# Moving the second pair of S5 output matmuls into the next unit, and writing the A blocks out

## The chip, the cores and the metric

The kernel runs on one core of one Trainium2 chip, as one program. The metric is device time in microseconds (us), the median of several runs; lower is better. PE is TensorE, DVE VectorE, ACT ScalarE, POOL GpSimd, SP the queue that issues most loads.

## The reference, cut to what matters

One layer of a hybrid decoder on 256 prompt rows and 8 x 8 sample rows, so 320 token columns, with a model width of 4096, all in fp32. One input projection feeds three branches, A (gated convolution), B (RG-LRU) and C (S5); their outputs are concatenated, projected back, gated and added to the input, and a last RMSNorm follows.

```python
proj = h @ w_in
a_b, a_c, a_x, a_g, b_x, b_g, c_u, c_g = _split_cols(proj)
conv_out, conv_a_new = _causal_dwconv(conv_a, a_c * a_x, w_conv_a, b_conv_a)
out_a = a_b * conv_out * jax.nn.silu(a_g)
...
bu_re = jnp.einsum('gpi,btgi->btgp', bb_re, u)      # S5: into 64 complex states per group
bu_im = jnp.einsum('gpi,btgi->btgp', bb_im, u)
...                                                 # diagonal complex scan over time: hr, hi
y = (jnp.einsum('gip,btgp->btgi', s5_c_re, hr) - jnp.einsum('gip,btgp->btgi', s5_c_im, hi)
     + s5_d * u).reshape(bn, t_len, W_C)            # second term: the skip term
y = jax.nn.gelu(y)
y = y * jax.nn.sigmoid(y @ w_glu + b_glu)
out_c = y * jax.nn.silu(c_g)
mixed = jnp.concatenate([out_a, out_b, out_c], axis=-1) @ w_out
```

## The kernel before, in words

Channels lie on the 128 partitions and tokens along the free axis. Each fp32 matmul of a projection is made of three fp32r matmuls (high x high, high x low, low x high). Weights stream in as slabs of 128 x 1024 words through a ring of four. For each slab SP issues the load, ACT copies the high part (`hi`, L575 to L582), DVE subtracts it to get the low part (`lo`, L877 to L880), and PE runs 24 matmuls on it (`slab`, L400 to L419). ACT and DVE prepare slabs three ahead of PE, so in their loops the index c runs from 3 to 18 where PE's runs from 0 to 15. A slab of the old ring place must be finished by PE before ACT may write that place.

The stages are: a head (L470 to L474, written out instruction by instruction: the projections whose results feed B and C, and the conditioning matmuls), then the A stage, then G (the GLU projection of C), B, and O (the output projection).

The change is in the **A stage**. It has eight units u of 16 slabs: two halves h, each with four units m (512 columns each of a_c, a_x, a_b and a_g), u = 4h + m. PE runs it as a loop of eight passes, ACT and DVE as loops of two passes (one per half) with the four units written out inside, POOL likewise. Beside the projection of A, each unit carries the S5 work of 128 channels of C, in four parts j = 0 to 3, t = 4u + j:

- PE, after slabs 1, 3, 6 and 9: six small matmuls into A0[0] and A0[1] (L488 to L490). The first of a unit waits for `bbu_ready`, the split operands UU_LO and BBU_LO that DVE writes at its c = 3 (L1111, L1112).
- DVE, at c = 5, 7, 10 and 13: `turn` (L1065 to L1081), which rotates by cosine and sine tables, and runs two scans; it ends with `q_done`.
- POOL, in order of t: six products and sums (L1337 to L1342) that rotate back into HRI[j % 2] and end with `hs5_done`; then a copy to the staged state and `frac` (L1296 to L1300), the fractions from which ACT makes the tables of part t + 2. Before HRI is written again, `y_done` must show that PE has read it. At the end of a unit POOL stores the state and waits for the store (L1351); for m = 2 it also stores the convolution state (L1355). At m = 2, before its last part, it waits for `conva_done` and copies that state (L1332, L1333). At the start of a unit it waits for `y_done` of all earlier pairs and loads CC, the output matrices (L1325). At the start of a half it first waits for `ag_done` and fills PADA's borders (L1290, L1291, `pada_ready`).
- PE, after slab 8 (parts 0 and 1) and after slab 15 (parts 2 and 3): the **output matmuls** (L501, two instructions for each of four fp32 matmuls) into A0[2]. Each pair waits for its `hs5_done`; the first also for `cc_ready` (ACT has negated the imaginary half, L694) and `y_sum` (DVE has read A0[2] of the unit before).
- DVE, after its last slab of the unit: waits for `y_done` of the second pair and adds the skip term (L1123, L1124, `y_sum`).

For the A branch, ACT evacuates the four banks at the unit's end (L720 to L725). DVE runs the convolution in four `conv_a` calls at m = 2, c = 4, 8, 11 and 14 (L1083 to L1097), and two products at m = 3. In a half's last unit, ACT at c = 5 waits for `y_sum` and runs GELU over three finished rows of C and SiLU over four gate rows (L704, L706). DVE begins a half with a wait for `pada_ready`.

After the A stage, G's first slab on PE waits for Y_LO, which DVE writes once `frac_done` has reached 34, that is after POOL's last `frac` (L1130 to L1138).

Within the two-pass loops the wait values and the column addresses depend on h, so they come from registers; outside they are constants.

Of the kernel before, what the change touches and what calls it, by code (L numbers as in the profile page):

```python
# [47 lines left out]
N_A, N_G, N_O = 8, 2, 8  # L48
# [17 lines left out]
SW = TP + DB * (DS + 1)  # L66
# [6 lines left out]
C_BRG, C_BIG, C_LAM, C_BGLU, C_S5D, C_GF = 240, 256, 272, 288, 296, 304  # L73
# [35 lines left out]
def build(nc, a):  # L109
    ctx = ExitStack()  # L110
    with ctx:
# [71 lines left out]
        CC = at("s5_cc", s + 2048, 2, BLK, 32)  # L183
# [213 lines left out]
        def _(pe):  # L397
# [76 lines left out]
                pairs(n)  # L474


            with pe.Fori(0, N_A) as u:
                for c in range(SPG):
                    slab(SLAB_A + u * SPG, c, KT, Q_A + u, H_HI, H_LO, T, after_head=True)
                    if c in (1, 3, 6, 9):  # L480
                        j = c // 3
                        if j == 0:
                            pe.wait_ge(bbu_ready, u + 1)
                        pe.wait_ge(bu_used, 4 * u + j + 1)
                        r = slice(32 * j, 32 * j + 32)
                        for n in range(2):
                            out = A0[n][:, 0:SW]
                            mm(out, BBU_HI[r, n, :], UU_HI[r, :], start=True, stop=False)  # L488
                            mm(out, BBU_HI[r, n, :], UU_LO[r, :], start=False, stop=False)
                            last = mm(out, BBU_LO[r, n, :], UU_HI[r, :], start=False, stop=True)  # L490
                        last.then_inc(bu_done, 1)
                    if c in (8, 15):
                        pair = c // 15
                        if pair == 0:
                            pe.wait_ge(cc_ready, u + 1)
                            pe.wait_ge(y_sum, u + 1)
                        pe.wait_ge(hs5_done, 4 * u + 2 * pair + 2)
                        for n in range(2):
                            for par in range(2):
                                j = 2 * pair + par  # L500
                                last = mm(A0[2][32 * j:32 * j + 32, 0:SW], CC[:, n, j, :], HRI[par][:, n, :],  # L501
                                          start=n == 0, stop=n == 1)
                        last.then_inc(y_done, 1)


            with pe.Fori(0, N_G) as g:
# [61 lines left out]
        def _(act):  # L568
            fn = nc.scalar.activation
            st = act_step  # L570
# [106 lines left out]
            tables(0, 0)  # L677
            act.wait_ge(hdv_free, N_H - HSL)
            act.wait_ge(ada_used, CHUNKS * KT)
            with act.Fori(0, 2) as h:  # L680
                st.enter(h, 32)
                for m in range(4):
                    u = 4 * h + m
                    nb = SLAB_A + u * SPG
                    q = Q_A + u
                    for c in range(AHEAD, AHEAD + SPG):
                        if c == 3:
                            act.wait_ge(bu_done, 4 * u + 1)
                            fn(UU_HI[:], CST[:, u, :], ACT.Copy)
                            fn(BBU_HI[:], BB[:, u], ACT.Copy).then_inc(bbu_hi_done, 1)  # L690
                        hi(nb, c)
                        if c == 5:
                            act.wait_ge(cc_in, 16 * (u + 1))
                            fn(CC[:, 1], CC[:, 1], ACT.Copy, scale=-1.0).then_inc(cc_ready, 1)  # L694
                        if c in (3, 6, 9, 12):
                            j = c // 3 - 1
                            act.wait_ge(q_done, 4 * u + j + 1)
                            fn(COEF[:], MASK[:], ACT.Copy, scale=MAGF[:, 0, bass.ds(4 * u + j, 1)]).then_inc(
                                coef_done, 1)
                        if m == 3 and c == 5:  # L700
                            act.wait_ge(y_sum, 4 * h + 3 + 1)
                            act.sem_inc(act_passed, 1)
                            rows = CST[:, bass.ds(4 * h, 3), :]
                            fn(rows, rows, ACT.Gelu_apprx_tanh)  # L704
                            rows = SG[:, bass.ds(4 * h, 4), :]
                            fn(rows, rows, ACT.Silu).then_inc(silu_done, 1)  # L706
                        if c in (6, 9, 12, 15):
                            j = c // 3 - 2
                            tables((j + 1) % 2, 4 * u + j + 1)
                    for b in range(BLK):  # L710
                        if b == 0 and m == 0:
                            act.wait_ge(pada_ready, h + 1)
                        if b == 0 and m == 2:
                            act.wait_ge(conva_done, h + 1)
                            act.wait_ge(staged_a, h + 1)
                        if b == 0 and m == 3:
                            act.wait_ge(ab_done, h + 1)
                        bank_ready(q, b, nb + SPG)
                        if m == 0:
                            fn(PADA[:, b, 2:2 + TP], M[:, b, 0:TP], ACT.Copy)  # L720
                            fn(PADAS[:, b, :, 2:], MS[:, b], ACT.Copy).then_inc(bank_free, 1)
                        elif m == 1:
                            fn(AROW[:, 4 * h + b, :], M[:, b, 0:T], ACT.Copy).then_inc(bank_free, 1)
                        else:
                            fn(TMPA[:, b, :], M[:, b, 0:T], ACT.Copy).then_inc(bank_free, 1)  # L725
                act.wait_ge(bank_free, 4 * (Q_A + 4 * h + 3) + 8)
                fn(TMPA[:], TMPA[:], ACT.Silu).then_inc(silu_a_done, 1)
            st.leave(2)


            act.wait_ge(silu_done, 2)
# [135 lines left out]
        def _(dve):  # L867
# [15 lines left out]
            def col(c):  # L883

                return PAR[:, bass.ds(c, 1)] if not isinstance(c, int) else PAR[:, c:c + 1]
# [213 lines left out]
                    then(ins)  # L1099


            with dve.Fori(0, 2) as h:
                st.enter(h, 16 * 4 + 4 * 4 - 1)
                dve.wait_ge(pada_ready, h + 1)
                for m in range(4):
                    u = 4 * h + m
                    nb = SLAB_A + u * SPG
                    for c in range(AHEAD, AHEAD + SPG):
# [6 lines left out]
                            conv_a(h, c // 3 - 1)  # L1115
                        if c in (5, 7, 10, 13):
                            turn(4 * u + c // 3 - 1, (c // 3 - 1) % 2)
                        if m == 3 and c == 4:
                            dve.wait_ge(conva_done, h + 1)
                            dve.wait_ge(bank_free, freed(Q_A + 4 * h + 2, 3))  # L1120
                            rows = AROW[:, bass.ds(4 * h, BLK), :]
                            tt(rows, rows, TMPA[:], MUL).then_inc(ab_done, 1)
                    dve.wait_ge(y_done, 2 * u + 2 + 1)  # L1123
                    stt(CST[:, u, :], CST[:, u, :], col(C_S5D + u), A0[2][:, 0:SW], MUL, ADD).then_inc(y_sum, 1)  # L1124
                    if m == 3:
                        dve.wait_ge(ab_done, h + 1)
                        dve.wait_ge(silu_a_done, h + 1)
                        rows = AROW[:, bass.ds(4 * h, BLK), :]
                        tt(rows, rows, TMPA[:], MUL).then_inc(ag_done, 1)
            st.leave(2)  # L1130


            dve.wait_ge(staged_s, 8)
# [387 lines left out]
```

## Time and profile before

| what | value |
|---|---|
| median of 3 runs | 2037.04 us (2034.55 to 2037.42) |
| the profiled execution | 2038.62 us, span 2037.0 us, mean granted clock 0.977 |
| PE busy | 1932.3 us (95% of the span) |
| DVE, ACT, POOL busy | 1133.0, 809.6, 430.6 us (56%, 40%, 21%) |
| DMA | 472.25 MB, mean 232 GB/s |
| chain that ended last | PE 79%, POOL 6%, issue 5%, DVE 5%, DMA 3% |

PE is the engine to watch: what PE waits for, and what a wait then does to the granted clock, is what stands between this kernel and a shorter one. The chain of work that ended last is nearly all PE, but 6% of it lies on POOL, which is busy for 21% of the span only, all of it between 644 and 1206 us (the A stage). A time on a row is the start in us from the span's start; the bracket at its end is how long the engine had been idle and what ended that.

### The profile page before, as it was taken

How to read it: one execution, taken by the hardware profiler on the slowest of the kernel's cores; microseconds unless marked ns; L12 is line 12 of the kernel's file. 1: busy time of each engine (PE TensorE's matmuls, PEld its weight loads, DVE VectorE, ACT ScalarE, POOL GpSimd, SP SyncE). 2: the span in 40 equal slices, each digit the busy share in tenths (PEclk: the TensorE clock that was granted, in tenths of full speed). 3: DMA queues.
4: the chain of work that ended last, by engine and by line, in shares of the span. 5: the costliest groups of instructions: out<-in, count | busy, mean ns of one | idle time of the engine just before them, and what ended most of it. 6: DMA issues, size and time to landing. Idle time of an engine off the chain costs nothing.

```text
span 2037.0 us, 37797 instructions
## 1 busy us (share of the span) xinstructions
PE 1932.3 (95%) x14410; PEld 1758.1 (86%) x14410; DVE 1133.0 (56%) x1535; ACT 809.6 (40%) x1076; POOL 430.6 (21%) x499
## 2 busy tenths in 40 slices
PE   4899999999999999899999889999989999999995
PEld 0688888888888999798998889999978899899995
DVE  2556667555454767776669656655743323333444
ACT  2343323322223444344444445677743223323332
POOL 1000000000001776676676660000000000000000
PEclk9899999999999999899999999999989999999998
DMA  9999999999997443333442434544467767677543
GB/s 388 375 374 353 365 356 352 344 350 344 351 365 296 128 138 133 116 117 128 138 135 96 138 129 160 170 159 158 140 225 262 273 234 273 238 272 258 176 145 124
DMA packets 132054, 472.25 MB, mean 232 GB/s; under 512 B 15424, under 2 KB 18432, under 8 KB 131920
## 3 DMA queue, kind: packets, MB, share of 16 engines
q1 hardware_dynamic: 125712, 448.38, 61.2%
q0 software_dynamic: 4480, 16.01, 2.1%
q10 hardware_dynamic: 1728, 6.07, 0.8%
q8 instruction: 84, 1.38, 0.3%
q14 instruction: 50, 0.41, 0.1%
HBM read 461.68 MB, written 8.72 MB: 231 GB/s over the span
## 4 chain that ended last, share of the span: by engine, by line
PE 79%; POOL 6%; issue 5%; DVE 5%; DMA 3%; ACT 1%; POOLq 0%; DVEq 0%; SPq 0%; ACTq 0%
PE m L414 16%; PE m L415 15%; PE m L416 15%; PE m L458 8%; PE m L459 7%; PE m L460 7%; PE aux L428 6%; DMA ada<-in_ada 3%; PE aux L556 2%; PE aux L520 1%; POOL s_tmpp L1341 1%; POOL s_tmpp L1338 1%; PE aux L501 1%; DVE w_lo L880 1%; POOL sin L1297 1%
## 5 line engine op out<-in xcount | busy, mean ns | idle before, releaser
L414 PE MATMUL m<-h_hi,w_hi 128*128 128x320 f32 x2560 | 809.4, 316 | 14.5 <-issue 9.7
L415 PE MATMUL m<-h_lo,w_hi 128*128 128x320 f32 x2560 | 796.0, 311 | 0.0
L416 PE MATMUL m<-h_hi,w_lo 128*128 128x320 f32 x2560 | 795.9, 311 | 0.0
L880 DVE TENSOR_TENSOR w_lo<-w_raw,w_hi 128x1024 fp32r<-128x1024 f32 x325 | 414.2, 1293 | 497.7 <-ACT w_hi L582 497.0
L582 ACT ACTIVATE w_hi<-w_raw 128x1024 fp32r<-128x1024 f32 x325 | 339.7, 1055 | 540.8 <-PE m L416 540.3
L414 PEld LDWEIGHTS m<-h_hi,w_hi 128*128 128x128 f32 x2560 | 485.5, 190 | 52.1 <-issue 42.6
L415 PEld LDWEIGHTS m<-h_lo,w_hi 128*128 128x128 f32 x2560 | 485.8, 190 | 0.8
L416 PEld LDWEIGHTS m<-h_hi,w_lo 128*128 128x128 f32 x2560 | 485.4, 190 | 0.0
L458 PE MATMUL m<-h_hi,w_hi 128*128 128x320 f32 x1024 | 324.1, 316 | 6.2 <-DVE h_lo L935 6.2
L460 PE MATMUL m<-h_hi,w_lo 128*128 128x320 f32 x1024 | 317.3, 310 | 0.0
L459 PE MATMUL m<-h_lo,w_hi 128*128 128x320 f32 x1024 | 317.3, 310 | 0.0
L597 ACT ACTIVATE w_hi<-w_raw 128x1024 fp32r<-128x1024 f32 x131 | 138.8, 1060 | 339.9 <-PE m L460 332.5
L458 PEld LDWEIGHTS m<-h_hi,w_hi 128*128 128x128 f32 x1024 | 193.0, 188 | 33.4 <-issue 32.2
L459 PEld LDWEIGHTS m<-h_lo,w_hi 128*128 128x128 f32 x1024 | 193.1, 189 | 0.0
L460 PEld LDWEIGHTS m<-h_hi,w_lo 128*128 128x128 f32 x1024 | 193.1, 189 | 0.0
L893 DVE TENSOR_TENSOR w_lo<-w_raw,w_hi 128x1024 fp32r<-128x1024 f32 x131 | 160.4, 1225 | 57.5 <-ACT w_hi L597 57.1
L428 PE MATMUL aux<-ada,c_T 128*32 128x256 f32 x2304 | 152.8, 400 | 30.6 <-DMA ada<-in_ada 30.6
L428 PEld LDWEIGHTS aux<-ada,c_T 128*32 128x32 f32 x2304 | 66.2, 111 | 97.6 <-DMA ada<-in_ada 41.5
L1307 POOL DMA_DIRECT2D part_b<-b_x x8 | 4.5, 566 | 606.2 <-DVE b_x L948 606.2
L947 DVE TENSOR_TENSOR b_x<-b_x,m 128x512 f32<-128x512 f32 x56 | 38.5, 688 | 103.0 <-PE m L460 102.9
L1407 POOL DMA_DIRECT2D x<-in_x x8 | 4.3, 534 | 330.5 <-PE m L416 330.5
L556 PE MATMUL aux<-gate_ring,c_T 128*32 128x256 f32 x768 | 52.5, 390 | 8.8 <-DMA gate_ring<-in_ada 8.8
(251 smaller groups left out, 1664.8 us busy)
## 6 DMA issues: line engine op xcount, KB each, us to landing
w_raw<-in_w SPq DMA_DIRECT2D x456, 512.0 KB, 4.6
ada<-in_ada SPq DMA_DIRECT2D x288, 512.0 KB, 6.4
gate_ring<-in_ada SPq DMA_DIRECT2D x96, 512.0 KB, 5.5
x_head<-in_x ACTq DMA_DIRECT2D x8, 640.0 KB, 13.7
x<-in_x POOLq DMA_DIRECT2D x8, 640.0 KB, 5.6
out_y<-x SPq DMA_DIRECT2D x6, 640.0 KB, 3.5
part_b<-b_x POOLq DMA_DIRECT2D x8, 344.0 KB, 6.2
pad_b<-part_b POOLq DMA_DIRECT2D x4, 688.0 KB, 5.4
```

The source lines that it names most:

```text
L414: mm(out, w_hi, hi[:, k, :], start=k == 0, stop=False)
L415: mm(out, w_hi, lo[:, k, :], start=False, stop=False)
L416: last = mm(out, w_lo, hi[:, k, :], start=False, stop=k == nk - 1)
L428: last = mm(A0[bank][32 * r:32 * r + 32, 0:CW], CT[:, k, :], ADAX[slot][:, r, :], start=k == 0, stop=k == KT - 1)
L458: mm(out, w_hi, H_HI[:, k, :], start=kk == 0, stop=False)
L459: mm(out, w_hi, H_LO[:, k, :], start=False, stop=False)
L460: last = mm(out, w_lo, H_HI[:, k, :], start=False, stop=kk == HK - 1)
L556: last = mm(A0[0][32 * r:32 * r + 32, 0:CW], CT[:, k, :], ADA2[:, k % RING, r, :], start=k == 0, stop=k == KT - 1)
L582: fn(W_HI[:, c % RING], RAW[:, c % RING].rearrange("p (k n) -> p k n", k=2), ACT.Copy).then_inc(w_hi_done, 1)
L597: fn(W_HI[:, w_slot(n)], RAW[:, n % RING].rearrange("p (k n) -> p k n", k=2), ACT.Copy).then_inc(w_hi_done, 1)
L880: tt(W_LO[:, c % RING], RAW[:, c % RING].rearrange("p (k n) -> p k n", k=2), W_HI[:, c % RING].bitcast(F32), SUB).then_inc(w_lo_done, 1)
L893: tt(W_LO[:, w_slot(n)], RAW[:, n % RING].rearrange("p (k n) -> p k n", k=2), W_HI[:, w_slot(n)].bitcast(F32), SUB).then_inc(w_lo_done, 1)
```

## The change

Three edits. (1) PE's loop over the eight units is written out, and the second pair of output matmuls of unit u goes from behind slab 15 of unit u to behind slab 1 of unit u + 1, just ahead of that unit's first S5 input matmuls; the last unit's stays at the end. (2) What depends on it follows: DVE adds the skip term of unit u - 1 at c = 5 of unit u, after `turn`; ACT negates CC at c = 7 (was 5); GELU and SiLU come at c = 8 (was 5). (3) ACT's and DVE's two-pass loops are written out, so that their wait values and addresses are constants; POOL keeps its loop.

```diff
+            def s5_in_(u, j):
+                if j == 0:
+                    pe.wait_ge(bbu_ready, u + 1)
+                pe.wait_ge(bu_used, 4 * u + j + 1)
...
+                last.then_inc(bu_done, 1)
+            def s5_out(u, pair):
+                if pair == 0:
+                    pe.wait_ge(cc_ready, u + 1)
+                    pe.wait_ge(y_sum, u + 1)
+                pe.wait_ge(hs5_done, 4 * u + 2 * pair + 2)
...
+                last.then_inc(y_done, 1)
-            with pe.Fori(0, N_A) as u:
+            for u in range(N_A):
                 for c in range(SPG):
                     slab(SLAB_A + u * SPG, c, KT, Q_A + u, H_HI, H_LO, T, after_head=True)
+                    if c == 1 and u > 0:
+                        s5_out(u - 1, 1)
                     if c in (1, 3, 6, 9):
-                        j = c // 3
...
-                    if c in (8, 15):
-                        pair = c // 15
...
+                        s5_in_(u, c // 3)
+                    if c == 8:
+                        s5_out(u, 0)
+            s5_out(N_A - 1, 1)
@@ ACT
-            with act.Fori(0, 2) as h:
-                st.enter(h, 32)
+            for h in range(2):
...
-                        if c == 5:
+                        if c == 7:
                             act.wait_ge(cc_in, 16 * (u + 1))
                             fn(CC[:, 1], CC[:, 1], ACT.Copy, scale=-1.0).then_inc(cc_ready, 1)
...
-                        if m == 3 and c == 5:
+                        if m == 3 and c == 8:
                             act.wait_ge(y_sum, 4 * h + 3 + 1)
-                            act.sem_inc(act_passed, 1)
                             rows = CST[:, bass.ds(4 * h, 3), :]
                             fn(rows, rows, ACT.Gelu_apprx_tanh)
@@ DVE
+            def add_skip(u):
+                dve.wait_ge(y_done, 2 * u + 2 + 1)
+                stt(CST[:, u, :], CST[:, u, :], col(C_S5D + u), A0[2][:, 0:SW], MUL, ADD).then_inc(y_sum, 1)
-            with dve.Fori(0, 2) as h:
-                st.enter(h, 16 * 4 + 4 * 4 - 1)
+            for h in range(2):
...
                         if c in (5, 7, 10, 13):
                             turn(4 * u + c // 3 - 1, (c // 3 - 1) % 2)
+                        if c == 5 and u > 0:
+                            add_skip(u - 1)
...
-                    dve.wait_ge(y_done, 2 * u + 2 + 1)
-                    stt(CST[:, u, :], CST[:, u, :], col(C_S5D + u), A0[2][:, 0:SW], MUL, ADD).then_inc(y_sum, 1)
+                    if u == N_A - 1:
+                        add_skip(u)
```

## Rows read from the trace of the kernel before

**Rows 1.** Waits of PE: line, releaser, total us, times, longest us.
```profile
PE aux L501 <- POOL s_h__104 L1342: 14.8, 8, 5.2
...
PE m L414 <- issue: 9.7, 2, 4.9
...
PE m L414 <- DVE y_lo L1137: 4.7, 1, 4.7
PE aux L488 <- DVE s_bb_unit_lo L1112: 3.5, 2, 3.0
```
**Rows 2.** Timeline of PE, end of unit 2: start, duration, line, tiles, idle before.
```profile
852.02 0.31 PE L416 MATMUL m<-h_hi,w_lo 128*128 128x320 f32 x1
857.20 0.76 PE L501 MATMUL aux<-s_h__103,s_cc 128*32 128x328 f32 x1 [4.87 <-POOL s_h__104 L1342]
...
859.53 0.63 PE L414 MATMUL m<-h_hi,w_hi 128*128 128x320 f32 x1
```
**Rows 3.** Windows: PE, PEld, DVE, ACT, POOL busy us (instructions), clock, DMA.
```profile
855.00:860.00 5.00, 2.80 (x10) 1.03 (x11) 0.24 (x1) 0.00 (x0) 3.88 (x9) 0.50 0.18 74
```
**Rows 4.** Timeline of PE, ends of units 0 and 1.
```profile
719.78 0.46 PE L501 MATMUL aux<-s_h__103,s_cc 128*32 128x328 f32 x1 [0.54 <-POOL s_h__104 L1342]
...
721.01 0.41 PE L414 MATMUL m<-h_hi,w_hi 128*128 128x320 f32 x1
...
784.09 0.46 PE L501 MATMUL aux<-s_h__103,s_cc 128*32 128x328 f32 x1
...
785.32 0.42 PE L414 MATMUL m<-h_hi,w_hi 128*128 128x320 f32 x1
```
**Rows 5.** Timeline of POOL from unit 2 into unit 3.
```profile
847.21 1.07 POOL L1332 COPY stage_a<-pad_a 128x36 f32<-128x36 f32 x1 [6.53 <-DVE acts L1093]
...
856.27 0.87 POOL L1342 TENSOR_TENSOR s_h__104<-s_h__104,s_tmpp 128x328 f32<-128x328 f32 x1 [0.18 <-POOL s_tmpp L1341]
...
867.27 0.54 POOL L1325 DMA_DIRECT2D s_cc<-in_s5c  x1 [3.27 <-DMA out_o_ca<-stage_a]
875.09 0.90 POOL L1337 TENSOR_TENSOR s_h__103<-q,cos 128x328 f32<-128x328 f32 x1 [7.28 <-DVE q L1081]
```
**Rows 6.** Timeline of POOL from unit 6 into unit 7.
```profile
1142.35 0.54 POOL L1325 DMA_DIRECT2D s_cc<-in_s5c  x1 [3.32 <-DMA out_o_ca<-stage_a]
1150.80 0.89 POOL L1337 TENSOR_TENSOR s_h__103<-q,cos 128x328 f32<-128x328 f32 x1 [7.91 <-DVE q L1081]
```
**Rows 7.** Timeline of DVE inside a convolution call of unit 2.
```profile
830.55 0.95 DVE L1089 TENSOR_SCALAR acts<-pad_a,par 128x256 f32 x1 [0.20 <-DVE pad_a L1088]
```
**Rows 8.** Timeline of DVE and PE, first S5 part of unit 3.
```profile
867.62 0.41 PE L488 MATMUL aux<-s_u_unit_hi,s_bb_unit_hi 32*128 32x328 f32 x1
...
868.72 0.41 PE L414 MATMUL m<-h_hi,w_hi 128*128 128x320 f32 x1
...
873.99 0.82 DVE L1081 TENSOR_TENSOR_SCAN q<-s_coef,q 128x328 f32<-128x328 f32 x1
```
**Rows 9.** Timelines of POOL, DVE, PE and ACT where the halves meet.
```profile
922.79 1.64 POOL L1342 TENSOR_TENSOR s_h__104<-s_h__104,s_tmpp 128x328 f32<-128x328 f32 x1 [0.18 <-POOL s_tmpp L1341]
...
935.15 0.50 DVE L1111 TENSOR_TENSOR s_u_unit_lo<-acts,s_u_unit_hi 128x328 fp32r<-128x328 f32 x1 [7.25 <-POOL pad_a L1291]
...
936.04 0.42 PE L488 MATMUL aux<-s_u_unit_hi,s_bb_unit_hi 32*128 32x328 f32 x1 [3.02 <-DVE s_bb_unit_lo L1112]
...
928.38 1.28 ACT L689 ACT_TABLE_LOAD   x1 [2.66 <-issue]
```
**Rows 10.** Timelines of POOL and PE at the end of the A stage.
```profile
1198.78 1.64 POOL L1342 TENSOR_TENSOR s_h__104<-s_h__104,s_tmpp 128x328 f32<-128x328 f32 x1 [0.18 <-POOL s_tmpp L1341]
...
1204.40 0.88 POOL L1300 TENSOR_TENSOR sin<-sin,cos 128x328 f32<-128x328 f32 x1 [0.18 <-POOL cos L1299]
...
1206.45 0.64 PE L414 MATMUL m<-y_hi,w_hi 128*128 128x328 f32 x1 [4.68 <-DVE y_lo L1137]
```
**Rows 11.** DMA queues of the page: packets, MB, share of 16 engines.
```profile
q8 instruction: 84, 1.38, 0.3%
```

More of the change, by code:

```diff
@@ L474, in _ @@
                 pairs(n)
-            with pe.Fori(0, N_A) as u:
+            def s5_in_(u, j):
+                if j == 0:
+                    pe.wait_ge(bbu_ready, u + 1)
+                pe.wait_ge(bu_used, 4 * u + j + 1)
+                r = slice(32 * j, 32 * j + 32)
+                for n in range(2):
+                    out = A0[n][:, 0:SW]
+                    mm(out, BBU_HI[r, n, :], UU_HI[r, :], start=True, stop=False)
+                    mm(out, BBU_HI[r, n, :], UU_LO[r, :], start=False, stop=False)
+                    last = mm(out, BBU_LO[r, n, :], UU_HI[r, :], start=False, stop=True)
+                last.then_inc(bu_done, 1)
@@ new lines, in s5_out @@
+            def s5_out(u, pair):
[3 more added lines that the diff above has]
+                pe.wait_ge(hs5_done, 4 * u + 2 * pair + 2)
+                for n in range(2):
+                    for par in range(2):
+                        j = 2 * pair + par
+                        last = mm(A0[2][32 * j:32 * j + 32, 0:SW], CC[:, n, j, :], HRI[par][:, n, :],
+                                  start=n == 0, stop=n == 1)
+                last.then_inc(y_done, 1)
@@ L478, in _ @@
+            for u in range(N_A):
                 for c in range(SPG):
                     slab(SLAB_A + u * SPG, c, KT, Q_A + u, H_HI, H_LO, T, after_head=True)
+                    if c == 1 and u > 0:
+                        s5_out(u - 1, 1)
                     if c in (1, 3, 6, 9):
-                        j = c // 3
[L482 to L491, printed above, removed]
-                    if c in (8, 15):
-                        pair = c // 15
[L494 to L503, printed above, removed]
+                        s5_in_(u, c // 3)
@@ L727, in _ @@
                 fn(TMPA[:], TMPA[:], ACT.Silu).then_inc(silu_a_done, 1)
-            st.leave(2)
             act.wait_ge(silu_done, 2)
@@ L1129, in _ @@
                         tt(rows, rows, TMPA[:], MUL).then_inc(ag_done, 1)
-            st.leave(2)
             dve.wait_ge(staged_s, 8)
```

## The prediction

> **What bounds the kernel now.** I read the list of PE's waits first, since PE is busy for 95% of the span. A wait of PE matters when nothing else would have held PE at that place a little later. The largest entry on which this change acts is L501, the output matmuls, which wait 14.8 us in eight places for POOL's last sum of a part [rows 1]. The timelines show where: 4.9 us at the end of unit 2, 5.2 at the end of unit 6 (the longest of the list), 0.54 at the end of unit 0, and nothing at the end of unit 1, where the first L501 follows the last slab without a bracket [rows 1, 2, 4]. So the two m = 2 units carry 10 of the 14.8 us, and what they lose is more than the bracket: in the window behind the wait the granted clock is 0.50, that is 1.2 GHz instead of 2.4, and an L501 takes 0.76 us instead of 0.46 [rows 2 to 4].
>
> Second, the timeline of POOL, because POOL ends those waits. In unit 2 POOL stands still for 6.5 us until DVE's last convolution call is done, then copies the convolution state and starts its last part at once [rows 5]. That ends at 857.14, and PE follows at 857.20. Then comes what decides the size of the gain: POOL stores two results, issues the load of CC at 867.27, and is free at 867.81; but it starts unit 3 only at 875.09, after 7.3 us of waiting for DVE's `turn` [rows 5]. That `turn` waited for PE's first S5 matmuls (L488 at 867.62), which come two slabs behind the pair that had waited for POOL [rows 2, 8]. So **PE waits for POOL, and POOL then waits for PE**: a ring through PE, DVE and POOL, closed once per m = 2 unit. Unit 7 shows it again: free at 1142.89, started at 1150.80 [rows 6].
>
> Third, the place where the halves meet. POOL ends unit 3 at 924.43; fractions, a store and PADA's borders follow, DVE waits for the borders, and PE's first S5 matmuls of unit 4 start at 936.04, after 3.0 us of waiting [rows 9]. From 924.43 to 936.04 it is 11.6 us. At the end of the stage POOL ends its last part at 1200.42 and its last fraction at 1205.28, and G's first matmul starts at 1206.45 [rows 10]: 6.0 us after the part. In both places POOL's end of the last part, and not PE's last slab, sets what follows.
>
> **The change, part by part.** The sum is made against the profiled execution, 2038.62 us (its span and 1.6 us around it); the median of the three runs is 2037.04, 1.6 lower, so the gain is then taken from the median.
>
> *The pair behind slab 1 of the next unit.* It is the same number of matmuls; a pair without a wait takes 784.09 to 785.32, 1.23 us, wherever it stands [rows 4]. What goes is the wait ahead of it. A unit without waits takes 721.01 to 785.32, 64.3 us [rows 4]; less four input groups of 1.10 [rows 8] and two pairs of 1.23 this is 57.4 for 16 slabs, so two slabs are 7.2 us. After unit 2 PE would go on at 852.2 (one step of 0.15 behind the row at 852.02) instead of 859.53 [rows 2], reach the pair at 859.4, and find POOL's part done at 857.14: no wait, with 2.2 us to spare. Unit 6 has the same pattern. At unit 0 the 0.54 us goes [rows 4].
>
> What is late next is POOL's own path, so the gain isn't 4.9 us plus the slow clock, but what POOL's start in unit 3 gains. POOL is free at 867.81, or 867.3 with the 0.5 of unit 0. DVE's `turn` must be done as well: PE starts unit 3 at 851.7, two slabs 7.2, the pair 1.2, and from L488 to the end of the second scan 874.81 - 867.62 = 7.2 [rows 8], gives 867.3. The two arrive together. So POOL starts at 867.3 instead of 875.1: **7.8 us, 0.5 of them from unit 0, 7.3 from unit 2**. From there to unit 4's first S5 matmuls the path is POOL's own, four parts (875.09 to 924.43, 49.3 us) and 11.6 us [rows 5, 9], and moves as a whole. The 3.0 us of L488 therefore stays: PE reaches that place at 851.7 + 64.3 + 8.4 = 924.4 plus what unit 3's first pair waits, POOL allows it at 867.3 + 49.3 + 11.6 = 928.2. Units 4 and 5 are PE's pace, so unit 6 gets the 7.8 us passed on. There POOL is free 7.9 us before its start [rows 6]; its last part, and with it G's start, moves by **7.9 us** more.
>
> *What follows on ACT and DVE.* The skip term at c = 5 stands behind `turn`, which already waited for L488; `y_done` is older by then, so it adds no wait, and its one instruction leaves the unit's end. Queued behind it on DVE are the low parts of later slabs, which PE needs three slabs on. `y_sum` comes later, but its readers are the first pair at slab 8 and GELU, which is moved to c = 8, after slab 4. CC's load now waits for the later `y_done`: unit 3's comes at 859.4 + 1.2 = 860.6, POOL asks at 867.27 [rows 5]; in units without a delay it is equally early or just in time. The negation at c = 7 instead of 5 gives CC's transfer two slabs more. GELU, SiLU and their table loads go from ahead of slab 6's high part to ahead of slab 9's, three slabs before PE wants it: nothing. If those covers went, each would cost at most one slab, 3.6 us, once per half.
>
> *Constants instead of registers.* In unit 2 DVE's path from its first `turn` to its last convolution call is what POOL waits for [rows 5]. Before each group that takes an address from a register there is a small gap, 0.20 us in a row where DVE depends on itself alone [rows 7]. Three calls with four such places and three `turn`s with one lie on the path: 15 places. At 0 to 0.20 us each this is 0 to 3.0 us per half; I take 0.1 each less one, **1.4 us per half, 2.8 in all**, since the nearest row has the largest of the gaps in a call. It counts fully, as POOL's last part, its stores and unit 3 move with it.
>
> *The written-out loops.* DVE's and ACT's jumps go. ACT's shows 2.66 us of issue before its first work of unit 4 [rows 9], but DVE was held by POOL's borders until 935.15 [rows 9], and POOL keeps its loop: worth nothing here, at most 2.7 us once. The Trainium skill ("Runtime: NRT & Kernel Launch", Instruction fetch mechanics) says that a taken branch to a target outside the two fetched pages stalls the engine until they are loaded, and prefers unrolling. By that rule alone the change would gain these 2.7 us; by the row of DVE it gains none of them, and the sum keeps none.
>
> Sum: 0.5 + 7.3 + 7.9 + 2.8 = 18.5 us. Profiled execution 2038.6 - 18.5 = 2020.1; median 2037.0 - 18.5, **2018.5 us**.
>
> **The rivals.** (a) *DVE and POOL slow each other.* The same POOL sum takes 0.87 us in one place and 1.64 in another [rows 5, 9]. A unit has 24 such products and sums; if the new phase makes half of them as slow as the slow one, 12 x 0.77 = 9.2 us are lost per half, and nothing is gained: 2037. Half of that gives 2028. For it: POOL now starts unit 3 when DVE has a denser queue. Against: both POOL's start and `turn` keep their distance to PE's slabs within a microsecond. The Trainium skill ("SBUF — State Buffer", Who interferes with whom) says that a DVE instruction with two SBUF inputs and a GpSimd one that reads SBUF exclude each other for a whole instruction; that speaks against bringing POOL's parts closer to DVE's `turn` and low parts, most of which read two SBUF tiles. The two durations agree with it; by it each meeting costs POOL the rest of a DVE instruction, which is what the 0.77 us price.
>
> (b) *POOL's start in unit 3 doesn't move*, because something other than `turn` holds it that the wait list hides behind it. Then only 0.5 us and part of the constants are won, about 1 to 2 us: 2035.5, no change. Against it: the bracket names DVE's scan both times [rows 5, 6].
>
> (c) *Slower: straight-line code on PE has to be fetched.* Two of PE's waits are for "issue", 4.9 us each [rows 1]. If each of the seven further units paid one such reload, 34 us would be lost: 2018.5 + 34 = 2053. It decides from 18.5 / 7 = 2.6 us per unit. Against it: the head runs thousands of matmuls written out, and the list has no issue wait of its matmuls; the instruction queue moves 1.38 MB in 84 packets, 0.3% of the DMA time [rows 1, 11].
>
> (d) *More than forecast*: all of the registers' 3.0 us per half, ACT's 2.7, and a shorter wait at L488, which takes its slow clock with it (3 us): 18.5 + 3.2 + 2.7 + 3 gives 2009.6.
>
> **How the numbers follow.** Forecast, 2012 to 2024: 0.70. Rival (a), 2024 to 2033 in the main: 0.14. (b): 0.06. (c): 0.04. (d), below 2012: 0.06. The range 2010 to 2028 takes the forecast, most of (d) and the better half of (a). A difference of 0.2%, 4.1 us, is about what a measurement of this kernel can tell from no change. Slower by more: (c), 0.04. Same: (b) and the worst of (a), 0.08. Faster: 0.88.
>
> **What would show it.** Right: no wait of L501 at a second pair but the last; L501 of unit 2 behind unit 3's slab 1 without a bracket and at 0.46 us; POOL's first part of units 3 and 7 within 0.5 us of the end of its CC load; the 3 us at unit 4's L488 still there. The constants are right if POOL's 6.5 us before L1332 ends 1 to 2 us earlier relative to unit 2's first `turn`. Wrong: POOL's 49.3 us for four parts of unit 3 grown (a); a bracket with DVE's scan of 5 us or more still at POOL's first part (b); "issue" between PE's slabs of the A stage (c).

## The result, and the profile after

| what | before | after |
|---|---|---|
| median | 2037.23 us (4 runs, 2034.55 to 2037.77) | 2014.29 us (4 runs, 2013.91 to 2015.75) |
| ratio, after to before | | 0.9885, 95% interval 0.9873 to 0.9897 |
| the profiled execution | 2038.62 us, span 2037.0 | 2015.75 us, span 2014.2 |
| mean granted clock | 0.977 | 0.982 |
| first S5 matmul of unit 0 to G's first matmul | 545.3 us | 521.0 us |

By the medians the change gains 22.9 us, by the ratio 23.4 (21.0 to 25.9). 18.5 us were forecast; the time lies in the range, 2010 to 2028. In the kernel after, L485 to L487 are the input matmuls (before: L488 to L490), L499 the output matmuls (L501), L1336 the load of CC (L1325), L1343 the copy of the convolution state (L1332), L1348 to L1353 POOL's six products and sums of a part (L1337 to L1342), L1308 the first wide operation of a fraction, 128x328 (L1297), L591 and L886 the high and low part of a slab (L582, L880).

PE's waits, kernel after (line, releaser, total us, times, longest us), which answer [rows 1]:

```profile
PE m L414 <- issue: 10.3, 2, 5.5
...
PE m L414 <- DVE y_lo L1148: 4.6, 1, 4.6
PE aux L485 <- DVE s_bb_unit_lo L1122: 4.0, 1, 4.0
PE aux L499 <- POOL s_h__104 L1353: 3.9, 6, 1.4
```

The output matmuls wait 3.9 us instead of 14.8. Gone too is a wait that [rows 1] leaves out, for DVE's low parts (kernel before):

```profile
PE m L414 <- DVE w_lo L880: 4.8, 4, 2.1
```

It stood in units 2 and 6 alone, 2.1 and 2.7 us. The waits at unit 4's first input matmuls and at G's first matmul stay, and so do the two of 5 us for issue, which stand in the O stage. (POOL's busy time before is not all in the A stage, as said at the start: 387 of its 431 us are.)

Timeline of PE, kernel after: the end of unit 2's second pair, now behind slab 1 of unit 3; the start of unit 4; the end of the stage. It answers [rows 2, 9, 10].

```profile
851.79 0.31 PE L416 MATMUL m<-h_hi,w_lo 128*128 128x320 f32 x1
852.02 0.46 PE L499 MATMUL aux<-s_h__103,s_cc 128*32 128x328 f32 x1
...
853.25 0.41 PE L485 MATMUL aux<-s_u_unit_hi,s_bb_unit_hi 32*128 32x328 f32 x1
...
917.99 0.44 PE L499 MATMUL aux<-s_h__104,s_cc 128*32 128x328 f32 x1
922.38 0.64 PE L485 MATMUL aux<-s_u_unit_hi,s_bb_unit_hi 32*128 32x328 f32 x1 [3.95 <-DVE s_bb_unit_lo L1122]
...
1175.51 0.46 PE L499 MATMUL aux<-s_h__103,s_cc 128*32 128x328 f32 x1 [1.37 <-POOL s_h__104 L1353]
...
1181.38 0.64 PE L414 MATMUL m<-y_hi,w_hi 128*128 128x328 f32 x1 [4.57 <-DVE y_lo L1148]
```

The pair of unit 2 has no bracket and takes 0.46 us instead of 0.76. Behind it the granted clock is now full, 2.4 GHz, where it was 0.50 in [rows 3] (window, kernel after: PE, PEld, DVE, ACT, POOL busy us, clock, DMA):

```profile
850.00:855.00 5.00, 5.00 (x33) 3.76 (x32) 4.11 (x5) 1.06 (x1) 4.45 (x3) 1.00 0.67 207
```

Timeline of POOL, kernel after, from unit 2 into unit 3 and from unit 6 into unit 7, which answers [rows 5, 6]:

```profile
838.50 1.07 POOL L1343 COPY stage_a<-pad_a 128x36 f32<-128x36 f32 x1 [0.96 <-DVE acts L1099]
...
847.18 0.94 POOL L1353 TENSOR_TENSOR s_h__104<-s_h__104,s_tmpp 128x328 f32<-128x328 f32 x1 [0.18 <-POOL s_tmpp L1352]
...
849.86 2.86 POOL L1308 TENSOR_SCALAR sin<-s_step,s_turn 128x328 f32<-128x328 f32 x1 [0.21 <-POOL s_turn L1307]
...
862.02 0.54 POOL L1336 DMA_DIRECT2D s_cc<-in_s5c  x1 [2.16 <-DMA out_o_ca<-stage_a]
862.58 0.90 POOL L1348 TENSOR_TENSOR s_h__103<-q,cos 128x328 f32<-128x328 f32 x1
...
1126.00 0.54 POOL L1336 DMA_DIRECT2D s_cc<-in_s5c  x1 [2.14 <-DMA out_o_ca<-stage_a]
1126.56 0.90 POOL L1348 TENSOR_TENSOR s_h__103<-q,cos 128x328 f32<-128x328 f32 x1
```

Behind its CC load POOL goes on at once, twice: the waits of 7.3 and 7.9 us are gone, so the ring is open. Two other things are new. POOL waits only 0.96 us for the last convolution call, where it waited 6.53. And from the end of unit 2's last part (848.12) to the end of the CC load (862.56) it takes 14.4 us, where it took 10.7.

**Where the time went.** Each stretch runs from PE's first input matmul of one unit to that of another, in profiled executions (us). The last stretch ends at G's first matmul.

| stretch | forecast | before | after | gain |
|---|---|---|---|---|
| unit 0 to 2 | 0.5 | 131.4 | 128.5 | 2.9 |
| unit 2 to 4 | 8.7 (7.3 + 1.4) | 143.5 | 133.6 | 9.9 |
| unit 4 to 6 | 0 | 131.7 | 130.4 | 1.2 |
| unit 6 to G | 9.3 (7.9 + 1.4) | 138.8 | 128.6 | 10.2 |
| A stage | 18.5 | 545.3 | 521.0 | 24.3 |
| ahead of the stage | 0 | 661.1 | 660.3 | 0.8 |
| behind the stage | 0 | 830.6 | 832.8 | -2.2 |

The stretches ahead of and behind the stage hold no edit. Over all kernels of this study they lie between 659.4 and 663.9, and between 827.9 and 832.8, so a difference of some 4 us there shows no effect of an edit.

### The profile page after: what moved, and what is told of

It reads as the page before. It is cut to its first block, busy times and chain, and to the rows that moved or that the text cites. A ratio compares the mean times of both kernels' runs of the same rounds, so it can differ in the third digit from the quotient of the medians.

```text
span 2014.2 us, 36924 instructions
## 1 busy us (share of the span) xinstructions
PE 1925.7 (96%) x14410; PEld 1754.6 (87%) x14410; DVE 1128.4 (56%) x1535; ACT 803.1 (40%) x1072; POOL 451.5 (22%) x499
## 4 chain that ended last, share of the span: by engine, by line
PE 79%; DVE 6%; POOL 6%; issue 4%; DMA 3%; ACT 1%; POOLq 0%; SPq 0%; DVEq 0%; ACTq 0%
PE m L414 15%; PE m L416 15%; PE m L415 15%; PE m L458 8%; PE m L460 8%; PE m L459 8%; PE aux L428 6%; PE aux L565 2%; DMA ada<-in_ada 2%; DVE w_lo L886 1%; POOL sin L1308 1%; PE aux L529 1%; POOL s_tmpp L1352 1%; POOL s_tmpp L1349 1%; DVE x L1279 1%
## 5 line engine op out<-in xcount | busy, mean ns | idle before, releaser
L886 DVE TENSOR_TENSOR w_lo<-w_raw,w_hi 128x1024 fp32r<-128x1024 f32 x325 | 419.3, 1308 | 505.2 <-ACT w_hi L591 504.7
L591 ACT ACTIVATE w_hi<-w_raw 128x1024 fp32r<-128x1024 f32 x325 | 339.5, 1055 | 538.7 <-PE m L416 538.5
```

The lines of the kernel that those rows point to most:

```text
L591: fn(W_HI[:, c % RING], RAW[:, c % RING].rearrange("p (k n) -> p k n", k=2), ACT.Copy).then_inc(w_hi_done, 1)
L886: tt(W_LO[:, c % RING], RAW[:, c % RING].rearrange("p (k n) -> p k n", k=2), W_HI[:, c % RING].bitcast(F32), SUB).then_inc(w_lo_done, 1)
```

## The experiments

The theory was a ring (PE waits for POOL, POOL then for PE) that opens when the pair moves, plus a small gain of constants on DVE's path. The rivals put it elsewhere: in the constants, in contention, in PE's code. The kernel after was timed beside a median of 2037.23. Those with only PE's loop, with both loops of ACT and DVE, with the move alone and with the followers put back ran beside one further set of runs of the kernel before (median 2038.81), the other three beside another (2036.75); ratios are to these. The last five columns are from the profiled executions, in us. Each is a single execution: the kernel before and the one with PE's loop written out, whose times agree, differ by 2.3 us in the A stage and by up to 1.5 in a stretch, so gains of 1 to 2 us in one stretch are not shown by these columns alone.

| kernel | median us | ratio (95%) | A stage | 0 to 2 | 2 to 4 | 4 to 6 | 6 to G |
|---|---|---|---|---|---|---|---|
| before | 2037.23 | | 545.3 | 131.4 | 143.5 | 131.7 | 138.8 |
| PE loop written out | 2036.01 | 0.9991 (0.9981 to 1.0001) | 543.0 | 131.4 | 143.3 | 131.0 | 137.3 |
| DVE loop written out | 2032.52 | 0.9975 (0.9965 to 0.9985) | 537.9 | 132.9 | 139.1 | 132.9 | 133.1 |
| ACT and DVE loops written out | 2028.90 | 0.9955 (0.9938 to 0.9971) | 534.8 | 131.4 | 137.9 | 132.7 | 132.8 |
| the move, loops kept | 2022.94 | 0.9925 (0.9909 to 0.9942) | 529.5 | 129.8 | 135.7 | 129.4 | 134.5 |
| after, negation and GELU at c = 5 | 2025.17 | 0.9938 (0.9918 to 0.9958) | 531.8 | 128.5 | 139.2 | 129.8 | 134.3 |
| after | 2014.29 | 0.9885 (0.9873 to 0.9897) | 521.0 | 128.5 | 133.6 | 130.4 | 128.6 |
| after, POOL written out | 2001.85 | 0.9820 (0.9804 to 0.9836) | 513.8 | 128.2 | 128.9 | 128.2 | 128.5 |
| the same, shorter POOL path | 2002.76 | 0.9822 (0.9805 to 0.9838) | 509.1 | 128.2 | 128.2 | 128.2 | 124.4 |

### Only ACT's and DVE's loops written out

```diff
-            with act.Fori(0, 2) as h:
-                st.enter(h, 32)
+            for h in range(2):
...
-            with dve.Fori(0, 2) as h:
-                st.enter(h, 16 * 4 + 4 * 4 - 1)
+            for h in range(2):
```

> The kernel before, with ACT's and DVE's two-pass loops written out (constant waits and addresses) and nothing moved; PE keeps its loop and its order. Ring theory (PE waits for POOL at the end of an m = 2 unit, POOL then waits for PE): the ring stays, only DVE's path in units 2 and 6 gets about 2 us shorter each and unit 0 some 2 us: 2037 - 6 = 2031, with the wait ahead of L501 at the end of unit 2 still 3 us or more and POOL still waiting 6 us or more for DVE's scan at the start of unit 3. Rival (the written-out loops are the larger share of the 22.9 us gained): 2025 or less.

Measured: 2028.90 us, 9.2 us by the ratio, against 2.8 of the forecast. The ring is still there, as the timelines of POOL and PE of this kernel show:

```profile
842.45 1.07 POOL L1327 COPY stage_a<-pad_a 128x36 f32<-128x36 f32 x1 [0.96 <-DVE acts L1090]
...
861.81 0.54 POOL L1320 DMA_DIRECT2D s_cc<-in_s5c  x1 [2.95 <-DMA out_o_ca<-stage_a]
869.48 0.89 POOL L1332 TENSOR_TENSOR s_h__103<-q,cos 128x328 f32<-128x328 f32 x1 [7.12 <-DVE q L1078]
```
```profile
852.04 0.46 PE L501 MATMUL aux<-s_h__103,s_cc 128*32 128x328 f32 x1 [3.07 <-POOL s_h__104 L1337]
```

PE still waits 3.1 us for POOL, and POOL 7.1 us for PE's next input matmuls by way of DVE. The waits of the output matmuls for POOL as a whole are no less than the 14.8 us before:

```profile
PE aux L501 <- POOL s_h__104 L1337: 15.2, 13, 3.1
```

The second pairs of the six units other than 2 and 6 now wait 1.0 to 1.4 us each, where three of them waited 0.5 before and three not at all. That goes against what is won in units 0 to 2 and 4 to 6, which gain nothing here. In the kernel after, where the pair is moved, none of them waits but the last.

What the constants did is to shorten DVE's path in unit 2: from the first input matmul to the end of the last convolution call it is 54.5 us before, 49.8 here, 49.5 after. That is 4.7 us and not 1.4. The three convolution calls on the path give 2.8 of it and the four `turn`s 1.7 (21.4 to 19.7 us). The w_lo waits of PE are gone here and with DVE's loop alone written out, while 3.6 us of them stay with the move alone. The next two views show the calls.

DVE's operations of the convolution calls in unit 2, 785 to 847 us, by form (busy us, mean ns | idle before), kernel before:

```profile
L1089 DVE TENSOR_SCALAR acts<-pad_a,par 128x256 f32 x4 | 2.5, 619 | 0.8 <-DVE pad_a L1088 0.8
...
L1090 DVE TENSOR_SCALAR acts<-pad_a,par 128x64 f32 x4 | 1.8, 451 | 0.0
L1088 DVE TENSOR_TENSOR pad_a<-pad_a,acts 128x64 f32<-128x64 f32 x4 | 1.6, 392 | 0.0
```

The same three of the kernel after:

```profile
L1095 DVE TENSOR_SCALAR acts<-pad_a,par 128x256 f32<-128x256 f32 x4 | 1.7, 430 | 0.1
L1096 DVE TENSOR_SCALAR acts<-pad_a,par 128x64 f32<-128x64 f32 x4 | 1.2, 299 | 0.0
...
L1094 DVE TENSOR_TENSOR pad_a<-pad_a,acts 128x64 f32<-128x64 f32 x4 | 0.9, 213 | 0.0
```

The idle time falls from 0.8 to 0.1 us, but the operations themselves become shorter too, the small TENSOR_TENSOR from 392 to 213 ns. Beside POOL a whole call takes 6.6 us before and 4.9 after; the first call of the unit, which has no POOL beside it, takes 3.07 and 2.66, so the gaps alone are 0.4 us a call. The other 1.3 us appear only beside POOL, and are read here as time in which a DVE instruction stood behind one of POOL. The other side of that exchange is POOL's (kernel before, the one with DVE's loop alone written out, and after, over the A stage; columns as above):

```profile
L1297 POOL TENSOR_SCALAR sin<-s_step,s_turn 128x328 f32<-128x328 f32 x32 | 29.9, 935 | 7.5 <-POOL s_turn L1296 7.5
```
```profile
L1295 POOL TENSOR_SCALAR sin<-s_step,s_turn 128x328 f32<-128x328 f32 x32 | 48.7, 1521 | 7.5 <-POOL s_turn L1294 7.5
```
```profile
L1308 POOL TENSOR_SCALAR sin<-s_step,s_turn 128x328 f32<-128x328 f32 x32 | 57.9, 1810 | 7.5 <-POOL s_turn L1307 7.5
```

The fraction's first wide operation takes up to twice as long: a DVE without gaps leaves POOL waiting while POOL's own gaps stay (7.5 us in all three). All nine kernels fall in line: 765 to 936 ns in the three where DVE and POOL both have loops, 1520 to 1810 in the four where POOL alone has one, 862 and 905 in the two where neither has. In unit 2 that cost nothing in front of the last part, because POOL had 6.5 us of waiting there; 0.96 of them are left. The Trainium skill ("SBUF — State Buffer", Who interferes with whom) says that the ports that DVE and GpSimd share are an exclusive lock, and that the order of issue, not the shape of the operation, decides who blocks. The rows agree: with only DVE's loop written out the same instructions changed from 392 to 214 ns on the one engine and from 935 to 1521 on the other.

### Only DVE's loop written out

```diff
-            with dve.Fori(0, 2) as h:
-                st.enter(h, 16 * 4 + 4 * 4 - 1)
+            for h in range(2):
```

> The kernel before with DVE's two-pass loop alone written out; ACT's and PE's loops kept, nothing moved. If the gain of the run with constants on both engines (9 us) sits on DVE, since its path from the first rotation to the last convolution call of unit 2 is what POOL waits for: 2028 to 2031, and the convolution calls beside POOL take 4.9 us instead of 6.6. If ACT's register work or its jump carries it: 2034 or more.

Measured: 2032.52 us, 5.1 by the ratio, somewhat less than expected. DVE's path in unit 2 is 49.7 us, all of the shortening. So some 3 to 4 of the 9.2 us are ACT's (by the medians 3.6, in the A stage 3.1). Timeline of ACT in unit 0, this kernel, where ACT keeps its loop:

```profile
669.06 0.57 ACT L698 ACTIVATE s_coef<-s_mask,s_mag_turn 128x328 f32<-128x328 f32 x1 [2.54 <-DVE q L1081]
669.64 1.28 ACT L671 ACT_TABLE_LOAD   x1
670.94 0.48 ACT L671 ACTIVATE cos<-sin 128x328 f32<-128x328 f32 x1
```

And with ACT's loop written out as well:

```profile
668.54 0.57 ACT L697 ACTIVATE s_coef<-s_mask,s_mag_turn 128x328 f32<-128x328 f32 x1 [1.44 <-DVE q L1078]
669.01 0.46 ACT L671 ACTIVATE cos<-sin 128x328 f32<-128x328 f32 x1
```

As a loop, ACT's code loads a table of 1.28 us ahead of the first cosine of each half (here, and at 941.20 in unit 4) and another at its start (L689); written out, none of these stands there. The load stands ahead of a slab's high part, so DVE's `turn` of the second part comes later too: its scan ends 20.2 us after PE's first input matmul here (680.76 - 660.54), and 17.2 with ACT written out (678.29 - 661.05). Unit 0's **first** pair, which waits 2.1 us for POOL in the kernel before, waits 1.45 with DVE's loop alone written out and 0.20 with ACT's as well; after the change it waits 0.19. The Trainium skill ("ScalarE activation tables: per-element evaluation and per-set limits", Table sets in the compiler and the runtime) says that the back end places the table loads per block. The rows agree: a load of L671 in each half while the loop is a block of its own, and none there when it isn't.

### Only the move, loops kept

In this kernel ACT and DVE keep their two-pass loops, so the second pairs of units 3 and 7, each the last of a half, stay at their unit's end.

```diff
-                    if c == 1 and u > 0:
+                    if c == 1 and u % 4 > 0:
                         s5_out(u - 1, 1)
...
-            s5_out(N_A - 1, 1)
+                if u % 4 == 3:
+                    s5_out(u, 1)
...
-            for h in range(2):
+            with act.Fori(0, 2) as h:
+                st.enter(h, 32)
```

> The changed kernel with ACT's and DVE's two-pass loops kept, so waits and addresses come from registers again; PE is written out; the pairs of units m = 0 to 2 stand behind slab 1 of the next unit, that of m = 3 stays at its unit's end with its skip term. Ring theory: the move alone is worth the forecast 15 to 16 us (0.5 + 7.3 + 7.9): 2021, and together with the gain of the run with constants alone it gives about the whole 22.9. Rival (the written-out loops are the larger share): 2027 or more.

Measured: 2022.94 us, 15.3 by the ratio, where the forecast's terms for the move give 15.7. POOL starts unit 3 directly behind the CC load, as predicted (timeline of POOL):

```profile
866.49 0.54 POOL L1342 DMA_DIRECT2D s_cc<-in_s5c  x1 [2.15 <-DMA out_o_ca<-stage_a]
867.05 0.91 POOL L1354 TENSOR_TENSOR s_h__103<-q,cos 128x328 f32<-128x328 f32 x1
```

So the move opens the ring without the constants. That 867.05 lies so near the 867.3 of the prediction is luck, though: this execution comes to unit 2's first input matmul 3.1 us earlier than the one before (PE's timelines, this kernel, then before).

```profile
789.47 0.41 PE L485 MATMUL aux<-s_u_unit_hi,s_bb_unit_hi 32*128 32x328 f32 x1
```
```profile
792.55 0.41 PE L488 MATMUL aux<-s_u_unit_hi,s_bb_unit_hi 32*128 32x328 f32 x1
```

Counted from that matmul, POOL's start moves by 5.0 us (82.5 to 77.6), where 7.3 were forecast. The wait of 7.3 is gone, but POOL's last part of unit 2 takes 9.9 us instead of 7.7, and the two small copies behind it 1.25 and 1.19 instead of 0.21 and 0.19. The windows of that last part show what stands beside it (before, then this kernel; length first, then the columns of [rows 3]):

```profile
849.44:857.14 7.70, 2.88 (x20) 2.62 (x18) 2.96 (x2) 4.17 (x9) 7.16 (x7) 0.84 0.77 268
```
```profile
845.45:855.32 9.87, 9.62 (x66) 9.35 (x64) 8.96 (x7) 5.11 (x10) 9.34 (x7) 1.00 0.75 246
```

Before, PE stood still for most of it and DVE was busy for 3.0 of the 7.7 us; now PE goes on, and DVE is busy for 9.0 of 9.9. So the ring's wait had also kept DVE out of POOL's way, and that goes with it. In unit 6 the part and the copies are as slow, and the two stores are waited for 2.3 us longer as well (3.75 and 3.92 us, before 2.07 and 3.32), so POOL's start moves by only 2.2 us of 7.9.

The stretches show the same. Units 2 to 4 gain 7.8 us (7.3 forecast), of which 2.6 are unit 3's four parts, shorter than before (49.3 to 46.8); unit 6 to G gains only 4.2 (7.9 forecast); and units 0 to 2 and 4 to 6 together gain 3.8, for which 0.5 was forecast. So the 15.3 meet the 15.7 by misses that cancel. With the constants, 15.3 + 9.2 = 24.5 against 23.4 for both, within the intervals; by stretches the two do not simply add (units 2 to 4: 7.8 + 5.6 against 9.9).

### The followers put back

```diff
-                        if c == 7:
+                        if c == 5:
                             act.wait_ge(cc_in, 16 * (u + 1))
...
-                        if m == 3 and c == 8:
+                        if m == 3 and c == 5:
```

> The changed kernel with ACT's negation of CC back at c = 5 and GELU and SiLU back at c = 5; all else as changed. If the followers matter: in units 3 and 7 POOL asks for CC at 862 while PE is already at slab 2, so ACT, held at c = 5 until CC lands some 3 us later and then by 4.9 us of GELU and SiLU, gives slab 6's high part about 3 us late; PE waits there, the tables of the second part come late and POOL with them: 3 to 5 us per half, 2020 to 2024. If only the place of the pair matters: 2014.

Measured: 2025.17 us, 10.8 of the 23.4 us lost. Timelines of ACT and PE in unit 3, this kernel:

```profile
864.47 0.31 ACT L702 ACTIVATE s_cc<-s_cc 128x128 f32<-128x128 f32 x1 [11.13 <-DMA s_cc<-in_s5c]
864.80 1.28 ACT L711 ACT_TABLE_LOAD   x1
...
869.63 1.04 ACT L591 ACTIVATE w_hi<-w_raw 128x1024 fp32r<-128x1024 f32 x1
```
```profile
871.98 0.62 PE L414 MATMUL m<-h_hi,w_hi 128*128 128x320 f32 x1 [1.91 <-DVE w_lo L886]
...
888.69 0.44 PE L499 MATMUL aux<-s_h__103,s_cc 128*32 128x328 f32 x1 [2.87 <-POOL s_h__104 L1353]
```

With the negation at c = 5, ACT stands 11.1 us for CC's load, which POOL issues only after its stores, and then makes GELU and SiLU (4.8 us) before it may go on with a slab. PE waits 1.9 us for that slab. The larger loss is behind it: DVE's `turn` of part 1 stands behind the late low part, its scan ends at 879.7 instead of 871.1, POOL's second part ends 5.9 us later (888.5 against 882.6) with everything on POOL's path behind it, and the first pair waits 2.9 us. In the kernel after, the negation waits 2.05 us for the same load and GELU stands ahead of a slab that isn't due yet. The two moves were not taken apart, so which of them carries how much stays open.

### Only PE's loop written out

```diff
-            with pe.Fori(0, N_A) as u:
+            for u in range(N_A):
```

> The kernel before with PE's loop over the eight A units written out and nothing else: the cost or gain of straight-line code on PE. My forecast and the ring theory: nothing, 2037 within 2 us. Rival (c) of the prediction (each further unit pays a reload of 4.9 us): 2071 or so, and at least a wait for issue between slabs of the A stage. If PE's jump cost something that the trace doesn't show as a wait: a few us less than 2037.

Measured: 2036.01 us, 0.9991 (0.9981 to 1.0001), so no change. Of the two readings below, the first is PE's wait for issue in this kernel (as before, the two of the O stage), the second its instruction queue (packets, MB, share), against 84 packets in [rows 11]:

```profile
PE m L414 <- issue: 10.3, 2, 5.7
```
```profile
q8 instruction: 107, 1.75, 0.4%
```

The 23 further packets of code cost nothing that these runs can tell, and neither did the loop's own jumps.

### POOL's loop written out too, and a shorter path on POOL

By the profile after, what is left is POOL's path. The first kernel is the kernel after with POOL's loop written out as well:

```diff
-            with pool.Fori(0, 2) as h:
-                st.enter(h, 4 * (4 * 8 - 1))
+            for h in range(2):
```

> The changed kernel with POOL's two-pass loop written out as well, so that all waits and addresses of the A stage are constants; order as changed. POOL's 30 dependent steps of a unit stand 0.17 to 0.26 us apart, 5.8 us in unit 2. If register work makes half of these, POOL's path shortens by about 3 us per unit, and in units 2 to 4 and 6 to G, where POOL sets the pace, that shows: 2006 to 2009. If the 0.18 us are POOL's own step from one instruction to a dependent one: 2014 within 2 us, but for the jump where the halves meet (1 to 2 us).

Measured: 2001.85 us, some 12 below the kernel after, more than expected. The fraction's first wide operation over the A stage (columns as above; 1810 ns and 7.5 us of idle time in the kernel after):

```profile
L1308 POOL TENSOR_SCALAR sin<-s_step,s_turn 128x328 f32<-128x328 f32 x32 | 27.6, 862 | 3.4
```

POOL's gaps before such operations are halved, and its operations stand less behind DVE's. DVE pays for it, with its own gaps still gone: its small TENSOR_TENSOR of the convolution calls, 213 ns in the kernel after, now takes longer than the 392 of the kernel before (DVE by form, 785 to 847 us), and the two calls beside POOL take 7.2 and 6.5 us instead of 4.9.

```profile
L1094 DVE TENSOR_TENSOR pad_a<-pad_a,acts 128x64 f32<-128x64 f32 x4 | 2.3, 565 | 0.0
```

So it is not the missing gaps by themselves that made DVE's operations short, but that only the other engine had gaps. Of PE's waits in the A stage these are left:

```profile
PE m L414 <- DVE y_lo L1148: 3.1, 1, 3.1
PE aux L499 <- POOL s_h__104 L1352: 3.0, 2, 2.5
```

The A stage is 7.2 us shorter in the profile. The rest of the 12 lies outside it in this execution, where stretches differ by some 4 us between kernels anyway, so not all of the 12 is shown to be the edit's.

The second kernel shortens POOL's path further: it doesn't wait for its stores at a unit's end, fills PADA's borders for the second half right behind unit 3, and leaves out the fractions and the table of parts that don't exist.

```diff
-                    wait(out_s, 16 * (u + 1))
...
-                        wait(out_a, 16 * (h + 1))
+                    if u == 3:
+                        wait(ag_done, 2)
+                        pad_a(1)
```

> The changed kernel with POOL's loop written out and its path shortened without less computation of the outputs: it no longer waits at a unit's end for its stores (the wait stands ahead of the next write of the staging tile), fills PADA's borders right behind unit 3's fractions, and leaves out the two fractions and the table of parts that don't exist. If POOL's path sets what is left of the A stage's waits (1 us at unit 3's first pair, 4.0 at unit 4's first input matmuls, 1.1 and 1.5 at unit 7's pairs, 4.6 ahead of G, and the slow clock behind the longer two): 2000 to 2005, with the waits at unit 4 and G gone or under 1.5 us. If PE, ACT or DVE take over as what is late: 2010 or more.

Measured: 2002.76 us, no further gain that can be told from none. The profile shows that the path did become shorter: the A stage is 509.1 us, and of PE's waits in it one is left, ahead of G, longer than the 1.5 us expected at most.

```profile
PE m L414 <- DVE y_lo L1148: 3.1, 1, 3.1
```

Three stretches of two units now take 128.2 us each, with no wait of PE in them: 64.1 a unit is PE's own pace here. Both kernels beat the kernel after, and are the fastest of this study.

## Why the prediction was right, and where it was not

**The ring: right as a mechanism, near in size by luck.** Its terms were 0.5, 7.3 and 7.9. All three signs named for it are there: no wait at a second pair but the last (1.37 us), L499 of unit 2 without a bracket at 0.46 us, POOL directly behind its CC load in units 3 and 7. Rival (b), that something else holds POOL, is out. But the move alone brought POOL's start only 5.0 us forward in unit 2 and 2.2 in unit 6. What the step had wrong is that POOL's last part and its way to the CC load would take as long as before: that part had run beside a DVE that mostly stood still, and with the wait gone it takes 9.9 us instead of 7.7. That the move gave 15.3 us all the same comes from gains where hardly any was forecast: 2.6 in unit 3's parts, 3.8 in units 0 to 2 and 4 to 6. They weren't traced further.

**The constants: mis-sized, in two ways.** The step counted gaps: 0.1 us in 14 places, 1.4 per half. The gaps are about that. What the step left out is that a gap on DVE lets POOL's next instruction in, and that DVE then waits for it; DVE's path shortened by 5.0 us in unit 2 and not by 1.4. No row shows that wait itself; it is read from the durations, which follow the gaps of either engine in all nine kernels. It also took the constants to be a matter of DVE's path only, where ACT's loop brought two table loads per half: writing it out was worth some 3 to 4 us, whose loads, gaps and jump were not taken apart. In the stretch with its jump ahead of unit 4, for which the sum kept none, the loop makes 1.1 us (units 2 to 4: 139.1 with it, 137.9 without). Alone the constants gave 9.2 us against 2.8.

**Why the stretch was nearly right all the same.** From unit 2's first input matmul to POOL's start of unit 3 the forecast was 7.3 + 1.4 = 8.7, and 8.8 were measured (82.5 to 73.8 us). The terms are others: DVE's path -5.0, the start of POOL's last part nearer to the end of the convolution by 1.0, POOL's last part slower by 0.7 and its way to the CC load by 3.8, the wait in the ring -7.3. Two misses cancelled there: DVE's gain was over three times as large as forecast, and POOL's last part and its way to the CC load paid most of the surplus back.

**A stretch that was taken as fixed.** Nothing was forecast for units 0 and 1 but 0.5 us, and 2.9 were gained. [Rows 1] counts L501's waits in eight places, and the prediction looked up only some of them; the third longest, 2.1 us at unit 0's first pair, went to 1.45 with DVE's constants and to 0.20 with ACT's as well. Units 4 to 6 gained 1.2, which is no more than two executions can differ by.

**The wait at L488 of unit 4: right.** It stays, 3.0 before and 4.0 us after, because PE arrives earlier and POOL's path decides: 10.9 us from the end of POOL's part to the matmul, against 11.6.

**The followers: moves right, the way of the loss wrong.** As moved, they cost nothing that shows. Lost cover was priced at one slab at most, 3.6 us, per cover and half. Put back together, the negation and the two activations lost 10.8 us for two halves, 5.4 each: more than one such price and less than two, and the two were not taken apart. The step counted the slab that PE waits for, which is 1.9 us here, and not DVE's `turn`, which is queued behind that slab's low part and is ahead of all of POOL's further work.

**Rival (a), contention: real, in another place.** POOL's four parts of unit 3 were named as the sign and did not grow (49.3 to 48.9 us). But unit 2's last part did, from 7.7 to 8.4 us (9.9 with the move alone), and the fractions, from 935 to 1810 ns for the first wide operation; both lie on the path between units 2 and 3. Rival (c) is out by the kernel with only PE written out. Rival (d), more than forecast, is where the result leans: its largest term, constants at full price, is the one that came true, though for another reason than the size of the gaps.

## What to carry to other kernels

Where engine A waits for B and B a little later for A, price the move by the second wait, since it is the one that goes; then walk on along the same engine to what is late next, here POOL's fractions and stores, and ask what will run beside it once nobody stands still. When a total agrees, count each stretch from its own start before calling the terms right. Where two engines slow each other as DVE and POOL do here, a small idle gap can be worth more than its length, because the other engine takes the slot: count the instruction that gets in, on both sides. When a step is moved, price lost cover by the whole queue behind the waiting instruction, not by the first thing that is late.

## What the runs showed of the hardware

Operations that take addresses or wait values from a loop's register have a gap ahead of them: on DVE 0.20 us in [rows 7] against 0.1 us for four calls together with constants; on POOL 7.5 us in 32 places against 3.4. With the gaps on one engine only, the other's operations are the short ones: POOL's wide operation takes 1810 ns and DVE's small one 213 in the kernel after, 862 and 565 with POOL written out too. The same DVE operation on 128 x 64 words (L1088 of the kernel before) took 0.21 us in one call and 0.92 in another. A table load of 1.28 us stood ahead of the first cosine of a half for as long as ACT's code was a loop. The two jumps of PE's three-pass loop in the O stage go with waits for issue of 4.6 to 5.7 us in all nine kernels, those of its loop in the A stage, where there is one, with none. And 23 more packets of straight-line code for PE cost no time that a run could tell.
